# mLSTM heads: value blocks by head for heads 6 and 7, PSUM pairs, four mixed banks, and a new order of the head steps

## The reference

```python
def mlstm_mixer(h, w_in, conv_w, conv_b, gate_b, head_gain, w_out):
    z = h @ w_in                     # q and k before a convolution, v, o, gates
    ...
    h_fwd = mlstm_chunkwise(q, k, v, g[0, 0], log_sigmoid(g[0, 1]))
    h_bwd = flip(mlstm_chunkwise(flip(q), flip(k), flip(v), ...))
    hs = rms_norm(h_fwd + h_bwd) * head_gain       # per head, 128 values
    return (sigmoid(o) * hs).reshape(B, S, 1024) @ w_out
```

## Time and profile before

| What | Value |
|---|---|
| Median of 3 runs | 2063.38 us (2062.54 to 2065.6) |
| Profiled execution | 2057.26 us, span 2055.6 us |
| TensorE busy | 2008.5 us (98%) |
| VectorE busy | 1197.1 us (58%) |
| ScalarE busy | 749.1 us (36%) |
| GpSimd busy | 905.4 us (44%) |

### The profile page before, as it was taken

One profiled execution on the slowest core, in us unless ns is written; L12 is line 12 of the kernel. 1 busy time (PEld: TensorE's weight loads), 2 busy tenths in 40 slices (PEclk: granted clock), 3 DMA queues, 4 the chain that ended last, 5 costly groups with the idle time before them and its releaser, 6 DMA issues.

```text
span 2055.6 us, 26015 instructions
## 1 busy us (share of the span) xinstructions
PE 2008.5 (98%) x10107; PEld 1676.4 (82%) x10107; DVE 1197.1 (58%) x1964; ACT 749.1 (36%) x1043; POOL 905.4 (44%) x500
## 2 busy tenths in 40 slices
PE   8999899999999999999999999999999899999998
PEld 6878788987888888877788788888898788888887
DVE  6454657646789895688578877516665752111112
ACT  5344534333513222447542122125353344222121
POOL 3422424754545444346244444445444345444442
PEclk9999999999999999999999999999999999999999
DMA  5332203516577862240348777423342023322321
GB/s 160 94 89 77 77 2 103 164 62 159 144 195 180 201 166 84 81 139 21 90 117 203 186 183 198 129 72 114 103 127 83 21 83 103 103 89 95 103 92 72
DMA packets 229648, 234.47 MB, mean 114 GB/s; under 512 B 7036, under 2 KB 224469, under 8 KB 229405
## 3 DMA queue, kind: packets, MB, share of 16 engines
q1 hardware_dynamic: 229040, 232.78, 40.3%
q10 hardware_dynamic: 492, 0.12, 0.0%
HBM read 230.61 MB, written 2.26 MB: 113 GB/s over the span
## 4 chain that ended last, share of the span: by engine, by line
PE 88%; DVE 6%; issue 2%; ACT 1%; DMA 1%; POOL 1%; SPq 0%; DVEq 0%; ACTq 0%
PE ps L2523 22%; PE ps L2525 21%; PE ps L2524 21%; PE ps L2574 7%; PE ps L2579 4%; DVE adacc L2045 2%; PE ps L3367 1%; PE ps L3029 1%; PE ps L2960 1%; POOL wL L695 1%; PE ps L3405 1%; PE ps L2811 1%; PE ps L2990 1%; PE ps L3373 1%; DVE ssum L1538 1%
## 5 line engine op out<-in xcount | busy, mean ns | idle before, releaser
L695 POOL TENSOR_TENSOR wL<-raw,wH 128x1024 fp32r<-128x1024 f32 (+2 forms) x320 | 769.3, 2426 | 982.0 <-ACT wH L874 916.9
L874 ACT ACTIVATE wH<-raw 128x2048 fp32r<-128x2048 f32 (+2 forms) x160 | 300.6, 1879 | 431.5 <-PE ps L2525 329.5
L2523 PE MATMUL ps<-uH,wH 128*128 128x512 f32 x1088 | 425.5, 391 | 3.4 <-DVE xT L1655 0.9
L2525 PE MATMUL ps<-uH,wL 128*128 128x512 f32 x1088 | 423.5, 389 | 0.0
L2524 PE MATMUL ps<-uL,wH 128*128 128x512 f32 x1088 | 423.3, 389 | 0.0
L2045 DVE SCALAR_TENSOR_TENSOR adacc<-adaw,adab,adacc 128x256 f32<-128x256 f32 x372 | 307.7, 827 | 12.9
L2523 PE MATMUL ps<-hnH,wH 128*128 128x512 f32 x728 | 287.7, 395 | 2.1 <-DVE xT L1657 1.7
L2525 PE MATMUL ps<-hnH,wL 128*128 128x512 f32 x728 | 283.7, 390 | 0.0
L2524 PE MATMUL ps<-hnL,wH 128*128 128x512 f32 x728 | 283.2, 389 | 0.0
L2523 PEld LDWEIGHTS ps<-uH,wH 128*128 128x128 f32 x1088 | 204.3, 188 | 47.4 <-issue 3.8
L2525 PEld LDWEIGHTS ps<-uH,wL 128*128 128x128 f32 x1088 | 204.2, 188 | 42.7
(11 more groups left out here) (501 smaller groups left out, 3041.0 us busy)
## 6 DMA issues: line engine op xcount, KB each, us to landing
raw<-in_ffn_w_dram SPq DMA_DIRECT2D x60, 1024.0 KB, 5.4
adaw<-in_ada_w_dram SPq DMA_DIRECT2D x192, 256.0 KB, 7.1
raw<-in_w_dram SPq DMA_DIRECT2D x32, 1024.0 KB, 5.7
raw<-in_w_in_dram SPq DMA_DIRECT2D x14, 1024.0 KB, 5.4
raw<-in_od_w_in_dram SPq DMA_DIRECT2D x12, 1024.0 KB, 5.3
raw<-in_w_xkv_dram SPq DMA_DIRECT2D x16, 512.0 KB, 3.6
raw<-in_ffn_w_dram SPq DMA_DIRECT2D x8, 768.0 KB, 4.4
raw<-in_ev_w_in_dram SPq DMA_DIRECT2D x5, 1024.0 KB, 5.3
```

Source lines behind the costliest of these rows:

```text
L695: nc.gpsimd.tensor_tensor(wL[n % 2][:, k0:k1, 0:c], raw[n % 2][:, k0:k1, 0:c], wH[n % 2][:, k0:k1, 0:c].bitcast(F32), ALU.subtract).then_i ...
L874: nc.scalar.activation(wH[n % 2][:, 0:kc, 0:c], raw[n % 2][:, 0:kc, 0:c], ACT.Copy).then_inc(w_hi, 1)
L2523: nc.tensor.matmul(out_ap, wh, xh, start=first, stop=False)
L2525: return nc.tensor.matmul(out_ap, wl, xh, start=False, stop=last)
```

## The change

1. Unit 12 is made by head: its first block is head 6, its second head 7, each for all 512 tokens, so that a block has 32 parts of three products with 128 columns. The generator gives the first block out in slices of 10, 10 and 12 parts, the second in four slices of 8. The slice ahead of states(h) is left out from head 5 on. So head 4 has three slices, heads 5 and 6 two each. `take_values` copies such a block in one instruction; head 7's is copied in VectorE's head 6, behind heads_out(6, 0).
2. PSUM is allocated as four pairs of banks. heads_out reads both banks of a pair at once: two small steps in place of four, and for d = 0 one product of 128x512 with a broadcast factor in place of four pieces.
3. VectorE's head_sums(h - 2) and normed_head(h - 3) stand ahead of heads_out(h, 0), and heads_out(h - 1, 1) behind the fourth `decayed`. In the tail heads_out(7, 0) stands ahead of mixed_low(0), and heads_out(7, 1) ahead of head_sums(5).
4. ScalarE's casts stand in heads 0, 2, 4 and 6; the last of them is that of unit n + 14. GpSimd's `low` stands in heads 0, 2 and 4.
5. The transposed heads take banks 2, 3, 4, 5 in turn; out_rows(7, 0) writes banks 4 and 5, all other rows banks 6 and 7. Head transposes 2 and 3 follow out_rows(7, 1). The waits are set to match.

```diff
-MIX_BANK = (4, 5, 4, 5, 4, 5, 6, 7)
+MIX_BANK = (2, 3, 4, 5, 2, 3, 4, 5)
 def head_banks(h, d):
-    return {(6, 1): (4, 5), (7, 1): (2, 3)}.get((h, d), (6, 7))
+    return {(7, 0): (4, 5)}.get((h, d), (6, 7))
...
-        ps = [ctx.enter_context(nc.psum_tensor(f"ps{i}", [P, S], F32)) for i in range(8)]
+        pairs = [ctx.enter_context(nc.psum_tensor(f"ps{i}", [P, 2, S], F32)) for i in range(4)]
+        ps = [pairs[i // 2][:, i % 2, :] for i in range(8)]
...
-                if h in (0, 3, 5):
+                if h in (0, 2, 4):
                     low(n + 11 + h // 2)
...
-                if h in (0, 3, 5):
+                if h in (0, 2, 4, 6):
                     high(n + 11 + h // 2)
                 if h >= 2:
                     head_squares(h - 2)
...
             mixed_high(1)
-            high(n + 14)
             head_squares(ML_H - 2)
...
+                if u == ML_H // 2 - 1:
+                    ins = nc.vector.tensor_copy(vx[:, :, 2 * u + half, 0:ML_V], ps[bank(bb)].rearrange("p (t v) -> p t v", t=TB))
+                else:
+                    for tb in range(2):
...
+                both = pairs[head_banks(h, d)[0] // 2][:, :, 0:258].rearrange("p b (a c) -> p b a c", a=2)
+                den, m = both[:, :, :, ML_V], mden[:, 0:4].rearrange("p (b a) -> p b a", b=2)
+                chain(nc.vector.scalar_tensor_tensor(out=m, in0=den, scalar=-1.0, in1=ecol[:, :, row].rearrange("p (b a) -> p b a", b=2),
+                                                     op0=ALU.mult, op1=ALU.max))
+                chain(nc.vector.tensor_tensor(m, den, m, ALU.max))
                 chain(nc.vector.reciprocal(mden[:, 4:8], mden[:, 0:4]))
...
+                if d == 0:
+                    ins = nc.vector.tensor_tensor(hs[:, :, h * P:(h + 1) * P].rearrange("p (b a) c -> p b a c", b=2), both[:, :, :, 0:ML_V],
+                                                  mden[:, 4:8].rearrange("p (b a o) -> p b a o", b=2, o=1).to_broadcast([P, 2, 2, ML_V]),
+                                                  ALU.mult)
...
-                    if x == (3 if tail else 5) and h:
+                    if x == 3 and h:
                         heads_out(h - 1, 1)
-                if not tail:
-                    heads_out(h, 0)
-                    if h < 6:
-                        take_values(V_FILL[0] + h, (h + 2) // 2, h % 2)
-                    if h >= 2:
-                        head_sums(h - 2)
-                    if h >= 3:
-                        normed_head(h - 3)
+                if h >= 2 and not tail:
+                    head_sums(h - 2)
+                if h >= 3 and not tail:
+                    normed_head(h - 3)
+                heads_out(h, 0)
+                if h < 5:
+                    take_values(V_FILL[0] + h, (h + 2) // 2, h % 2)
+                if h == 6:
+                    take_values(V_FILL[0] + 5, 3, 1)
             mixed_low(0)
             mixed_low(1)
+            heads_out(ML_H - 1, 1)
             head_sums(ML_H - 3)
-            heads_out(ML_H - 1, 0)
             normed_head(ML_H - 4)
             mixed_low(2)
             mixed_low(3)
-            heads_out(ML_H - 1, 1)
             head_sums(ML_H - 2)
...
+                        alone = u == 12
+                        wide, count = (P, 4 * KC) if alone else (UC, 2 * KC)
+                        cs = slice(c * P, (c + 1) * P) if alone else slice(0, UC)
+                        for x in range(count):
...
+                            ins = parts(ps[bank(b)][:, pos * wide:(pos + 1) * wide], (hnH[:, k, ts], hnL[:, k, ts]),
+                                        (wH[(n + u) % 2][:, k, cs], wL[(n + u) % 2][:, k, cs]), k == 0, k == KC - 1)
...
+                            if alone and c:
+                                if x % 8 == 7:
+                                    yield
+                            elif x in (count * 5 // 16 - 1, count * 10 // 16 - 1, count - 1):
                                 yield
...
                 scores(h + 1, 0)
-                next(beside, None)
+                if h < 5:
+                    next(beside, None)
...
                 next(beside, None)
-                if h == ML_H - 1:
-                    head_transposes(2)
-                    head_transposes(3)
                 out_rows(h, 1)
+            head_transposes(2)
+            head_transposes(3)
             head_transposes(4)
```

More of the change, by code:

```diff
@@ L2359, in take_values @@
                 dve.wait_ge(blk_done, bb + 1)
-                for tb in range(2):
-                    src = ps[bank(bb)][:, tb * UC:(tb + 1) * UC].rearrange("p (h v) -> p h v", h=2)
-                    ins = nc.vector.tensor_copy(vx[:, 2 * half + tb, 2 * u:2 * u + 2, 0:ML_V], src)
+                if u == ML_H // 2 - 1:
+                    ins = nc.vector.tensor_copy(vx[:, :, 2 * u + half, 0:ML_V], ps[bank(bb)].rearrange("p (t v) -> p t v", t=TB))
+                else:
+                    for tb in range(2):
+                        src = ps[bank(bb)][:, tb * UC:(tb + 1) * UC].rearrange("p (h v) -> p h v", h=2)
+                        ins = nc.vector.tensor_copy(vx[:, 2 * half + tb, 2 * u:2 * u + 2, 0:ML_V], src)
                 ins.then_inc(blk_taken, 1)
@@ L2422, in heads_out @@
                 row = h + 32 * d
[L2423 to L2427, removed]
@@ L2428, in heads_out @@
-                chain(nc.vector.reciprocal(mden[:, 4:8], mden[:, 0:4]))
[L2429 to L2436, removed]
+                both = pairs[head_banks(h, d)[0] // 2][:, :, 0:258].rearrange("p b (a c) -> p b a c", a=2)
@@ new lines, in heads_out @@
+                den, m = both[:, :, :, ML_V], mden[:, 0:4].rearrange("p (b a) -> p b a", b=2)
+                chain(nc.vector.scalar_tensor_tensor(out=m, in0=den, scalar=-1.0, in1=ecol[:, :, row].rearrange("p (b a) -> p b a", b=2),
+                                                     op0=ALU.mult, op1=ALU.max))
+                chain(nc.vector.tensor_tensor(m, den, m, ALU.max))
+                chain(nc.vector.reciprocal(mden[:, 4:8], mden[:, 0:4]))
+                if d == 0:
+                    ins = nc.vector.tensor_tensor(hs[:, :, h * P:(h + 1) * P].rearrange("p (b a) c -> p b a c", b=2), both[:, :, :, 0:ML_V],
+                                                  mden[:, 4:8].rearrange("p (b a o) -> p b a o", b=2, o=1).to_broadcast([P, 2, 2, ML_V]),
+                                                  ALU.mult)
+                else:
+                    for i in range(TB):
+                        dst = hs[:, i, h * P:(h + 1) * P]
+                        ins = nc.vector.scalar_tensor_tensor(out=dst, in0=both[:, i // 2, i % 2, 0:ML_V], scalar=mden[:, 4 + i:5 + i],
+                                                             in1=dst, op0=ALU.mult, op1=ALU.add)
@@ L3338, in values_beside @@
                         bank_free(b)
-                        for x in range(2 * KC):
+                        alone = u == 12
+                        wide, count = (P, 4 * KC) if alone else (UC, 2 * KC)
+                        cs = slice(c * P, (c + 1) * P) if alone else slice(0, UC)
+                        for x in range(count):
                             pos, k = x // KC, x % KC
[L3341 to L3344, removed]
+                            tb = pos if alone else 2 * c + pos
+                            ts = slice(tb * P, (tb + 1) * P)
+                            ins = parts(ps[bank(b)][:, pos * wide:(pos + 1) * wide], (hnH[:, k, ts], hnL[:, k, ts]),
+                                        (wH[(n + u) % 2][:, k, cs], wL[(n + u) % 2][:, k, cs]), k == 0, k == KC - 1)
+                            if x == count - 1:
                                 ins.then_inc(blk_done, 1)
-                            if x % 5 == 4 and x < 12 or x == 2 * KC - 1:
+                            if alone and c:
+                                if x % 8 == 7:
+                                    yield
+                            elif x in (count * 5 // 16 - 1, count * 10 // 16 - 1, count - 1):
                                 yield
@@ L3352, in out_rows @@
                 pe.wait_ge(l_a, 8 * h + 4 * d + 4)
-                if (h, d) == (6, 1):
+                if (h, d) == (7, 0):
                     pe.wait_ge(blk_taken, TAKEN[V_FILL[1]])
-                elif (h, d) == (7, 0):
-                    pe.wait_ge(l_h, 13)
                 elif (h, d) == (7, 1):
-                    pe.wait_ge(h_st, 3 * HG_H + ML_H)
+                    pe.wait_ge(l_h, 2 * ML_H - 2)
                 elif h or d:
@@ L3379, in states @@
                 hp = (h % 2) * 64
-                if h % 2 == 0 and h:
+                if h == 6:
+                    pe.wait_ge(blk_taken, TAKEN[V_FILL[0] + 5])
+                elif h == 7:
+                    pe.wait_ge(blk_taken, TAKEN[V_FILL[1]])
+                elif h % 2 == 0 and h:
                     pe.wait_ge(blk_taken, TAKEN[V_FILL[0] + h])
@@ L3415, in head_transposes @@
                 pe.wait_ge(n_h, j + 1)
[L3416 to L3419, removed]
```

(10 more changed lines are left out.)

## The result

The changed kernel takes 2082.28 us (median of 4 runs, 2080.83 to 2088.37), the kernel before 2062.96 beside it: a ratio of 1.0100, 95% interval 1.0086 to 1.0114. It is slower by 19.3 us; 18.7 was forecast. The profiled execution took 2088.37 us (span 2086.6), 31.1 more than the one shown of before. That is more than the medians differ, and why is part of what follows.

The account below looks back on a forecast made before the run. TensorE's work plus its holes in heads 6 and 7, with the lower clock behind them, was taken to bound the kernel. Terms 4.5 + 3.5 + 1.7 + 9.0 = 18.7 us gave 2082 us (profiled 2076), range 2071 to 2088.

Parts of the forecast that it names:

- The narrow products: Unit 12 on TensorE: 192 products of 128 columns at 0.112 us replace 96 at 0.12, 10.1 us more.
- Head 4: Before out_rows(4, 1): GpSimd's instructions hold VectorE's norm steps ahead of heads_out; hole of 3.5 us, plus 1.7 clock loss.
- Head 6: Before out_rows(6, 1): the cast waits for the last slice and delays squares, sums and heads_out(6, 0); hole of 6.85 us.
- The tail: Before transposes(4), with heads_out(7, 1) ahead of head_sums(5) and normed_head(4): hole of 3.0 us, where 2.85 was.
- heads_out: VectorE's call of 2.12 us becomes 1.3 for d = 0, 1.7 for d = 1; worth nothing in heads 0 to 3.
- The clock: Loss at 1.2 GHz on TensorE: 1.7 us after head 4's hole, 3.2 us after head 6's.
- That VectorE slips its steps in between GpSimd's: Rival: head 4 has little hole, -3.5 to -5.2 us, about 2077 us; chance 0.2.
- cheap narrow products: Rival: narrow products cost 0.06 to 0.08 us each, 4 to 10 us less work, 2072 to 2078 us; chance 0.1.
- the cast that doesn't reach TensorE: Rival in head 6: the cast's wait is met before the last slice; not slower, -1.5 us, 2062 us; chance 0.1.

Follow-up runs that it names:

- low late: Changed kernel with, in head 4 on GpSimd, gated_head(2) first and the low of unit n + 13 waiting until normed_head(1) is done: 2073.64 us.
- cast late: Changed kernel with the cast of unit n + 14 back behind mixed_high(1), not in head 6: 2074.08 us.
- Norms behind: Changed kernel with head_sums(h - 2) and normed_head(h - 3) behind heads_out(h, 0) in every head, the cast left in head 6: 2068.06 us.
- tail: Kernel of 2052.84 us (wide products, late cast, norms ahead only in heads 3, 5) with head_sums(5) and normed_head(4) ahead of heads_out(7, 1): 2051.90 us.
- Pairs only: Kernel before with PSUM pairs and the shorter heads_out, nothing else: 2061.31 us, before 2061.90.
- both late: Changed kernel with the edits of "cast late" and "low late" together, narrow products kept: 2062.03 us, before 2061.90.

## Why the prediction was right, and where its size was luck

**The narrow products** were right: 9.5 us by themselves, forecast 10.1 from rows 4. By the 81 ns of the Trainium skill (TensorE: Matmul & The Clock Gate, "Back-to-back issue gap") it would have been 4; the trace disagrees with it for fp32r pairs with 128 columns, at 0.111 us.

**Head 4** was right in place and size (3.29 us for 3.5), and that GpSimd's holds are needed for it is shown by "low late": with GpSimd's order in this head changed and nothing else, it was gone. The cast's part in it is argued. The Trainium skill (SBUF — State Buffer, "SBUF: two separate sides") says that the loser of the shared port pair blocks for the other's whole instruction, and the trace agrees, with 2.28 us for a step of 0.16 beside a half of `low`. L2452, which has one SBUF input, was held as well, 1.32 us, as the forecast had it for L2448. The sum over 512 elements ahead of it (L2447), which started beside the same `low`, was not: 0.69 us.

**Head 6** was right (6.74 us for 6.85), shown by "cast late". "Norms behind" shows that this hole also needs heads_out(6, 0) behind the norm steps; without that the cast costs a smaller one, 3.1 us in head 7, by way of GpSimd.

**The tail** was right (2.92 for 3.0). It is the place of heads_out(7, 1) that sets it, as the "tail" run shows. In trade, the 1.07 and 1.78 us holes of before went.

**heads_out**: 1.3 us for d = 0 and 1.7 for d = 1 were forecast; the trace has 0.6 + 0.69 and 0.6 + 1.13. Covered in heads 0 to 3, as said: no hole there.

**The clock** is the term that was mis-sized. The sum had 1.7 us after head 4's hole and 3.2 after head 6's, against 3.4 before, so +1.5. The profiled execution lost 13.6 us after the one and 4.1 after the other. It lost 1.7 more at the start of the stage, behind the 0.85 us hole: the prediction says that the holes are in heads 6 and 7 alone and leaves this one out, which cost nothing of the clock in the profile of before. In all it is +16.0 for +1.5, and the profiled execution took 2088 us where the forecast had 2076. Work and holes were forecast at 17.2 (18.7 less the 1.5) and measured as 15.4 in the profile. In the timed runs the clock made 3 to 6 of the 19.3 us and work and holes 13 to 16, by how the lower level inside the hole is counted. The two errors have opposite signs, so that the medians match to 0.6 us is in part luck, and says less than the match of each hole.

**The rivals.** That VectorE slips its steps in between GpSimd's (a small hole in head 4) fell, and so did cheap narrow products and the cast that doesn't reach TensorE.

How long the lower clock lasts after a hole stays open. With narrow products behind head 4's hole it was 27.3 us in two profiles, each of the slowest run of its kernel; with wide ones, behind a longer hole, 13.7 and 10.2. That points to what TensorE runs, but other profiles speak against it as the whole cause. "Pairs only" had 13.7 us where before had 6.8, behind a shorter hole and with the same products. Behind the 0.85 us hole at the start of the stage, which all thirteen profiles have, 3.4 us of it followed in eight and none in five. And the kernel before has mean clocks from 0.991 to 0.996 from run to run.

## What to carry to other kernels

Before a step is put ahead of what the busiest engine waits for, list what that step itself waits for in each iteration; here one cast every other head stood ahead of the squares, and GpSimd's long products held steps on 4 elements for 1.2 to 2.3 us each. Narrower blocks may fill a hole, but an fp32r product with half the columns kept 93% of the cost: what filled a hole of 3.65 us brought 9.5 us of work. Where TensorE is the bound, a hole costs more than its length: before, 6.5 us of holes took 5.1 us of clock with them, and "both late", with some 7 us more of work and holes together than before but one hole in place of three, takes the same time for the clock it keeps. How much clock a hole takes differed from run to run, so it is better given as a range.

## What the runs showed of the hardware that was not expected

- TensorE stayed at 1.2 GHz for some 27 us in which it was never idle after the restart, in two profiles (the changed kernel and "cast late"), where 6.8 us had followed a hole of 3.65 before.
- A hole of 0.85 us, the same in all thirteen profiles, was followed by 3.4 us at 1.2 GHz in eight of them and by none in five.
- The kernels here differ in one stage, and the mean clock of the whole execution lies between 0.987 and 0.999. At some 2055 us of span 0.001 of it is 2 us, more than the medians of "pairs only" (0.6 us) or "tail" (0.9 us) differ from the kernels they start from.
- Once GpSimd runs one instruction after another, each step of a chain on VectorE can be held by one of them: three steps in a row took 1.32, 2.28 and 1.19 us, and in "low late" 0.75, 0.16 and 0.16.
